# The value products of the second attention with the weights as the stationary side, their results turned back by transposes

## The chip, the cores and the metric

The kernel runs on one core of a Trainium2 chip. The metric is the device time of one execution in microseconds (us). A core has TensorE (PE, with its weight loads shown apart as PEld), VectorE (DVE), ScalarE (ACT) and GpSimd (POOL); the SP queue issues the transfers. The engines run on their own and wait for one another through semaphores.

## The reference, cut to what matters

Two transformer blocks run one behind the other on 512 tokens of width 1024. The change is in the first layer of the second block, which has 8 heads of forgetting attention ("fox") and 8 heads of sparse attention. Each of the latter adds three gated attentions: over compressed keys ("cmp"), over selected key blocks ("slc") and over a window ("win"). At 512 tokens all the selected blocks are taken and the window reaches over everything, so slc and win are causal attentions over all the keys before a token.

```python
s = jnp.einsum('bqhd,bkhd->bhqk', qi, k).astype(jnp.float32) * scale
s = s + ci[..., None] - c[:, :, None, :]
p = masked_softmax(s, kpos[None, :] <= t[:, None])
...
o_s = jnp.einsum('bgrqk,bgqkd->bqgrd', p_s.astype(dt), vg)
...
o_w = jnp.einsum('bgrqk,bkgd->bqgrd', p_w.astype(dt), vw)
return gi[..., 0:1] * o_c + gi[..., 1:2] * o_s + gi[..., 2:3] * o_w
```

The last product of each, probabilities times values, is the one that is changed. In all, a head has 512 queries, up to 512 keys and 64 channels.

## The kernel before

The function `attention` works through 16 steps of two heads each. Steps 0 to 7 alternate cmp and fox (cmp 0, fox 1, cmp 2, fox 3 and so on), steps 8 to 15 alternate slc and win. The order of the work is written out by hand, a loop over the steps on each engine.

On TensorE iteration s does three things. `turn` transposes the probabilities `z` of step s, 128x128 at a time (L2324; the cmp steps' at L2319), in pieces of four: five pieces in a fox, slc or win step, two in a cmp step. They go to two banks of PSUM in turn, and a piece waits until the piece two before it has been copied out. ACT copies pieces 0 and 2 and DVE copies 1, 3 and 4 into `w_T` (L2199). `scores` computes the scores of step s+2 (L2213 and L2214 for cmp, L2222 to L2224 for the rest). `mix` multiplies step s's turned probabilities `w_T` with the values (L2345, cmp at L2341).

In `mix` the values, 128 keys by 64 channels, are loaded as weights, and up to 512 columns of `w_T` are streamed past them. The two heads of a step use columns 0 to 63 and 64 to 127 of the array, so the result stands in bank 7 by channel: 128 channels by 512 tokens, as the next layer wants it. For slc, mix(s) leaves its sum in the bank, and the win step behind it adds onto it.

On DVE iteration s masks and lowers the scores of step s+1 (`lower`, L2261, on 128x512 down to 128x128), adds a win step's result to its block (`add`, L2369), copies its pieces, and computes the softmax weights of step s+1 (`weigh`, L2275 to L2284). On ACT iteration s computes the exponentials of one head of step s+1 (L2293), copies its pieces of step s, copies the result of step s-1 out of bank 7 (`keep`, L2399, fox and cmp), computes the exponentials of the other head and scales its share of both (L2394). At the end of iteration 2 ACT and DVE also split a weight panel into high and low halves (L234, L243). POOL scales the rest of `z` (L2435).

Weights, values and probabilities are in float32. The kernel's source has a matmul once; the trace shows two records (passes) for each float32 matmul and one for a transpose.

Of the kernel before, what the change touches and what calls it, by code (L numbers as in the profile page):

```python
# [22 lines left out]
P = 128  # L23
# [2096 lines left out]
def attention(k, a, heads, f):  # L2120
# [18 lines left out]
    for s, (kind, _) in enumerate(steps):  # L2139
        first_piece.append(len(pieces))  # L2140
        for i in range(2 if kind == "cmp" else len(piece_parts)):
            eng = ("act", "dve")[i] if kind == "cmp" else "act" if i in by_act else "dve"
            done[eng] += 1
            pieces.append((s, i, eng, done[eng]))
    out_bank, turn_bank = 7, 5
# [3 lines left out]
    def pieces_of(s):  # L2149
        return range(first_piece[s], first_piece[s + 1] if s + 1 < n_steps else len(pieces))  # L2150

    def first_of_head(s):
        return steps[s][0] != "win"

    def last_of_head(s):
        return steps[s][0] != "slc"
# [4 lines left out]
    heads_before = [sum(last_of_head(x) for x in range(s)) for s in range(n_steps + 1)]  # L2161
# [4 lines left out]
    top, total, weight = (f.sb(s, [P, slots, TT]) for s in ("top", "total", "weight"))  # L2166
    early_z = heads[:, 6, 0:2 * TT * 32].rearrange("p (e c) -> p e c", e=2)
# [69 lines left out]
    def lower(dve, u):  # L2237
# [4 lines left out]
        if s >= slots // 2:  # L2242
            dve.wait_ge(turned, first_piece[s - slots // 2 + 1])
# [53 lines left out]
    def rest(block, parts, last_panel):  # L2297
# [5 lines left out]
        def _(pe):  # L2303
            def turn(n):
# [22 lines left out]
            def mix(s, j):  # L2327

                kind, i = steps[s]
                if kind == "cmp" and j:  # L2330
                    return
                if j == 0:
                    for n in pieces_of(s)[-2:]:
                        pe.wait_ge(out_of_bank[pieces[n][2]], pieces[n][3])
                    if first_of_head(s) and heads_before[s]:
                        pe.wait_ge(kept, heads_before[s])
                first, final = first_of_head(s) and j == 0, last_of_head(s) and j in (0 if kind == "cmp" else TT - 1,)
                for e in range(2):
                    out = ps[rows_of(e), out_bank, :]
                    if kind == "cmp":  # L2340
                        last = pe.matmul(out, a.vc[:, i // 2, :], w_T[0:32, e, 0:T], start=first, stop=final)  # L2341
                        continue
                    v = {"fox": a.fv[:, j, (2 * i + e) * HD:(2 * i + e + 1) * HD] if kind == "fox" else None,
# [934 lines left out]
```

## Time and profile before

| | |
|---|---|
| three runs | 1986.31 us median (1984.85 to 1991.64) |
| the profiled execution | 1989.59 us, of which its span is 1987.9 us |
| TensorE, busy share of the span | 95% |
| VectorE, ScalarE, GpSimd, busy share | 46%, 38%, 11% |
| the 16 steps | from about 975 to 1115 us of the span |

The profile gives starts in us from the start of the span. A row of the timeline merges neighbouring instructions of one line: its second column reaches from the start of the first to the end of the last, and a record of TensorE reaches to where its result lands, so that records overlap. How fast they follow is read from starts.

### The profile page before, as it was taken

The numbers are of one execution on the slowest core, as the hardware profiler recorded it, in microseconds if no ns is written. First come the engines' busy times: TensorE is split into PE (matmuls) and PEld (weight loads), VectorE is DVE, ScalarE is ACT, GpSimd is POOL, SyncE is SP. The second block draws the span as 40 slices with busy tenths as digits, with TensorE's granted clock in tenths as the row PEclk, the third lists the DMA queues.
The fourth block names the chain that finished last, engine by engine and source line by source line (L and its number), as shares of the span: only waits on it lengthen the run. The fifth ranks groups of instructions, "written<-read, shape, count | busy, mean of one in ns | idle before, by whom it ended". The sixth has DMA issues, their size and how long they took to land. (4 is left out here: it accounts for less than half of the span.)

```text
span 1987.9 us, 32845 instructions
## 1 busy us (share of the span) xinstructions
PE 1893.6 (95%) x13761; PEld 1546.7 (78%) x13761; DVE 917.6 (46%) x1352; ACT 747.3 (38%) x1259; POOL 223.0 (11%) x305
## 2 busy tenths in 40 slices
PE   7999988789999999999979899999999999999998
PEld 6777777657888888778856687888889888888887
DVE  5346666555433344376358464334322453343223
ACT  6533444243321332254468453222222452222222
POOL 3013665100000000000234100000310000000000
PEclk9999999999999999999879999999999799999999
DMA  5322000012322322453100023322233113232221
GB/s 180 106 65 64 4 4 3 11 43 85 104 87 91 100 85 96 99 115 100 43 22 1 22 68 103 102 89 89 86 107 101 43 43 106 85 99 82 85 92 68
DMA packets 152068, 147.97 MB, mean 74 GB/s; under 512 B 13532, under 2 KB 149882, under 8 KB 151930
## 3 DMA queue, kind: packets, MB, share of 16 engines
q1 hardware_dynamic: 151804, 145.91, 23.6%
q8 instruction: 109, 1.79, 0.4%
q14 instruction: 29, 0.24, 0.0%
q10 hardware_dynamic: 126, 0.04, 0.0%
HBM read 143.84 MB, written 2.10 MB: 73 GB/s over the span
## 5 line engine op out<-in xcount | busy, mean ns | idle before, releaser
L243 DVE TENSOR_TENSOR weight_low<-weight_ring,weight_high 128x2048 fp32r<-128x2048 f32 (+2 forms) x141 | 301.1, 2136 | 486.0 <-ACT weight_high L234 485.9
L234 ACT CAST weight_high<-weight_ring 128x2048 fp32r<-128x2048 f32 (+2 forms) x141 | 249.8, 1773 | 322.9 <-PE psum L263 321.8
L261 PE MATMUL psum<-tail_operand_high,weight_high 128*128 128x512 f32 (+1 forms) x768 | 292.7, 381 | 6.4 <-DVE tail_operand_low L2762 5.7
L262 PE MATMUL psum<-tail_operand_low,weight_high 128*128 128x512 f32 (+1 forms) x768 | 290.4, 378 | 0.0
L263 PE MATMUL psum<-tail_operand_high,weight_low 128*128 128x512 f32 (+1 forms) x768 | 290.4, 378 | 0.0
L261 PE MATMUL psum<-tail_hidden_high,weight_high 128*128 128x512 f32 (+1 forms) x520 | 183.2, 352 | 2.5 <-DVE tail_hidden_low L3208 2.5
L263 PE MATMUL psum<-tail_hidden_high,weight_low 128*128 128x512 f32 (+1 forms) x520 | 182.7, 351 | 0.0
L262 PE MATMUL psum<-tail_hidden_low,weight_high 128*128 128x512 f32 (+1 forms) x520 | 182.5, 351 | 0.0
L261 PEld LDWEIGHTS psum<-tail_operand_high,weight_high 128*128 128x128 f32 x768 | 145.3, 189 | 38.0 <-DVE tail_operand_low L2762 5.2
L262 PEld LDWEIGHTS psum<-tail_operand_low,weight_high 128*128 128x128 f32 x768 | 145.5, 189 | 29.7 <-issue 0.5
L263 PEld LDWEIGHTS psum<-tail_operand_high,weight_low 128*128 128x128 f32 x768 | 145.5, 189 | 29.4
L261 PE MATMUL psum<-middle_operand_high,weight_high 128*128 128x512 f32 (+1 forms) x392 | 156.2, 398 | 0.8 <-DVE middle_part L1737 0.8
L263 PE MATMUL psum<-middle_operand_high,weight_low 128*128 128x512 f32 (+1 forms) x392 | 155.4, 396 | 0.0
L262 PE MATMUL psum<-middle_operand_low,weight_high 128*128 128x512 f32 (+1 forms) x392 | 155.3, 396 | 0.0
L261 PE MATMUL psum<-middle_hidden_high,weight_high 128*128 128x512 f32 x320 | 128.1, 400 | 4.6 <-DVE middle_hidden_low L1613 4.6
L262 PE MATMUL psum<-middle_hidden_low,weight_high 128*128 128x512 f32 x320 | 128.0, 400 | 0.0
L263 PE MATMUL psum<-middle_hidden_high,weight_low 128*128 128x512 f32 x320 | 127.8, 399 | 0.0
L261 PEld LDWEIGHTS psum<-tail_hidden_high,weight_high 128*128 128x128 f32 x520 | 98.3, 189 | 17.4 <-issue 2.7
L262 PEld LDWEIGHTS psum<-tail_hidden_low,weight_high 128*128 128x128 f32 x520 | 98.4, 189 | 14.7
L263 PEld LDWEIGHTS psum<-tail_hidden_high,weight_low 128*128 128x128 f32 x520 | 98.2, 189 | 14.5
L261 PEld LDWEIGHTS psum<-middle_operand_high,weight_high 128*128 128x128 f32 (+1 forms) x392 | 73.4, 187 | 19.7 <-DVE middle_part L1737 1.2
L2863 ACT CAST tail_hidden_high<-tail_gate 128x512 fp32r<-128x512 f32 x44 | 27.3, 621 | 162.0 <-DVE tail_gate L2891 162.0
(431 smaller groups left out, 3173.5 us busy)
## 6 DMA issues: line engine op xcount, KB each, us to landing
weight_ring<-in_w_ff SPq DMA_DIRECT2D x32, 1024.0 KB, 5.2
weight_ring<-in_ffn_w_gate SPq DMA_DIRECT2D x22, 1024.0 KB, 5.3
weight_ring<-in_ffn_w_up SPq DMA_DIRECT2D x22, 1024.0 KB, 5.3
weight_ring<-in_ffn_w_down SPq DMA_DIRECT2D x16, 768.0 KB, 4.4
weight_ring<-in_rw_in SPq DMA_DIRECT2D x11, 1024.0 KB, 5.3
weight_ring<-in_ffn_w_down SPq DMA_DIRECT2D x16, 640.0 KB, 3.9
weight_ring<-in_attn_w_in SPq DMA_DIRECT2D x9, 1024.0 KB, 5.4
weight_ring<-in_w_out SPq DMA_DIRECT2D x4, 1024.0 KB, 5.1
```

Of the source, the lines that this page charges most:

```text
L234: act.copy(self.w_hi[:, slot, 0:n], self.ring[:, slot, 0:n]).then_inc(self.panel_high, 1)
L243: dve.tensor_tensor(self.w_lo[:, slot, 0:n], self.ring[:, slot, 0:n], self.w_hi[:, slot, 0:n], ALU.subtract).then_inc(self.panel_low, 1)
L261: pe.matmul(out, w_hi, x_hi, start=start, stop=False)
L262: pe.matmul(out, w_hi, x_lo, start=False, stop=False)
L263: return pe.matmul(out, w_lo, x_hi, start=False, stop=stop)
L2863: act.copy(t.hidden_hi[:, i - 1 + m, :], gate[:, at, :]).then_inc(high, 1)
```

## The change

The two sides of the product trade places for the fox, slc and win steps. `mix` now loads a 128x128 part of `w_T` (128 keys by 128 tokens) as weights and streams the 64 channels of the values past it, once for each of the 10 pairs of a token tile and a key tile on or below the diagonal and for each of the two heads. The result stands in bank 7 by token: 128 tokens by 4 tiles of 128 channels. A step's sums are closed with the step, so slc and win meet no longer in the bank: ACT copies an slc step's result to `out_rows` (the tile `rstd`), and DVE adds the win step's to it.

The results of the 4 fox and the 4 win steps are then turned back to channels by four transposes each (`turn_rows`), which TensorE does in the next iteration, between `scores` and `mix`, and copied (fox, ACT, `keep_block`) or added (win, DVE, `add_block`) into their block. These pieces take a place of their own among the two PSUM banks of the pieces. cmp steps keep their form.

```diff
+        if s and steps[s - 1][0] in ("fox", "win"):
+            eng = "act" if steps[s - 1][0] == "fox" else "dve"
+            done[eng] += 1
+            pieces.append((s, "rows", eng, done[eng]))
...
+            def turn_rows(s):
+
+                n = rows_piece(s)
+                if n is None:
+                    return
+                pe.wait_ge(kept, s + 1)
+                _, _, who, shows = pieces[n - 2]
+                pe.wait_ge(out_of_bank[who], shows)
+                for t in range(TT):
+                    last = pe.transpose(ps[:, turn_bank + n % 2, t * P:(t + 1) * P], out_rows[:, t * P:(t + 1) * P], k.ident[:])
+                last.then_inc(turned, 1)
...
-                    last = pe.matmul(out[:, j * P:T], v, w_T[:, e, w_at[j]:w_at[j] + T - j * P], start=first, stop=final)
...
+                    for tile in range(TT):
+                        for e in range(2):
+                            at = ((2 * i + e) if kind == "fox" else i // 2) * HD
+                            for j in range(tile + 1):
+                                c = w_at[j] + (tile - j) * P
+                                last = pe.matmul(ps[:, out_bank, tile * P + e * HD:tile * P + (e + 1) * HD], w_T[:, e, c:c + P],
+                                                 v[:, j, at:at + HD], start=j == 0, stop=j == tile)
...
-                for j in range(TT):
-                    mix(s, j)
+                if s:
+                    turn_rows(s - 1)
+                mix(s)
+            turn_rows(n_steps - 1)
...
+                    dve.tensor_tensor(out_rows, ps[:, out_bank, :], out_rows, ALU.add).then_inc(kept, 1)
+
+            def add_block(s):
+                if steps[s][0] == "win":
+                    n, block = rows_piece(s), heads[:, block_of(s), :]
+                    dve.wait_ge(turned, n + 1)
+                    dve.tensor_tensor(block, ps[:, turn_bank + n % 2, :], block, ALU.add).then_inc(out_of_bank["dve"], 1)
...
+                    act.copy(heads[:, block_of(s), :] if steps[s][0] == "cmp" else out_rows, ps[:, out_bank, :]).then_inc(kept, 1)
+
+            def keep_block(s):
+                n = rows_piece(s)
+                if steps[s][0] == "fox":
+                    act.wait_ge(turned, n + 1)
+                    act.copy(heads[:, block_of(s), :], ps[:, turn_bank + n % 2, :]).then_inc(out_of_bank["act"], 1)
```

The order of the instructions on TensorE around an slc step's product, before (the names are result, streamed side, weights; the shape is that of the result):

```order
L2223 MATMUL psum<-attn_all_ks_high,attn_all_nq 128x256
L2224 MATMUL psum<-attn_all_ks_low,attn_all_nq 128x256
L2345 MATMUL psum<-attn_w_T,attn_all_vs 64x512 x2
L2345 MATMUL psum<-attn_w_T,attn_all_vs 64x384 x2
L2345 MATMUL psum<-attn_w_T,attn_all_vs 64x256 x2
L2345 MATMUL psum<-attn_w_T,attn_all_vs 64x128 x2
L2324 MATMUL psum<-identity,attn_z 128x128 x20
```

The same place in the changed kernel, behind a win step:

```order
L2226 MATMUL psum<-attn_all_ks_high,attn_all_nq 128x256
L2227 MATMUL psum<-attn_all_ks_low,attn_all_nq 128x256
L2316 MATMUL psum<-identity,rstd 128x128 x4
L2359 MATMUL psum<-attn_all_vs,attn_w_T 128x64 x20
L2339 MATMUL psum<-identity,attn_z 128x128 x20
```

Eight matmuls in four pairs have become 20, and the four transposes of the step before stand between the scores and them.

On ACT, the queue before in iteration 6 (a cmp step), from its piece copy on to the first exponentials of iteration 7:

```order
L2199 COPY attn_w_T<-psum 32x512
L2399 COPY mixer_mixed<-psum 128x512
L2293 ACTIVATE attn_z,attn_total<-attn_z,attn_top 128x512
L2293 ACTIVATE attn_z,attn_total<-attn_z,attn_top 128x384
L2293 ACTIVATE attn_z,attn_total<-attn_z,attn_top 128x256
L2293 ACTIVATE attn_z,attn_total<-attn_z,attn_top 128x128
L2394 ACTIVATE attn_z<-attn_z,attn_weight 128x512 x2
L2293 ACTIVATE attn_z,attn_total<-attn_z,attn_top 128x512
```

And the same stretch in the changed kernel:

```order
L2202 COPY attn_w_T<-psum 32x512
L2425 COPY rstd<-psum 128x512
L2296 ACTIVATE attn_z,attn_total<-attn_z,attn_top 128x512
L2296 ACTIVATE attn_z,attn_total<-attn_z,attn_top 128x384
L2296 ACTIVATE attn_z,attn_total<-attn_z,attn_top 128x256
L2296 ACTIVATE attn_z,attn_total<-attn_z,attn_top 128x128
L2417 ACTIVATE attn_z<-attn_z,attn_weight 128x512 x2
L2431 COPY mixer_mixed<-psum 128x512
L2296 ACTIVATE attn_z,attn_total<-attn_z,attn_top 128x512
```

The fox result goes to `rstd` first, and its copy into the block (`keep_block`, L2431) stands behind the scaling and ahead of everything of the next iteration.

On DVE, the last instructions of the 16 steps before, with the first ones of the stage behind them:

```order
L2199 COPY attn_w_T<-psum 128x512 x3
L2369 TENSOR_TENSOR mixer_mixed<-psum,mixer_mixed 128x512
L2453 UNCONDITIONAL_BRANCH
L3204 UNCONDITIONAL_BRANCH
L3208 TENSOR_TENSOR tail_hidden_low<-mixer_mixed,tail_hidden_high 128x512 x8
```

And in the changed kernel:

```order
L2202 COPY attn_w_T<-psum 128x512 x3
L2383 TENSOR_TENSOR rstd<-psum,rstd 128x512
L2389 TENSOR_TENSOR mixer_mixed<-psum,mixer_mixed 128x512
L2487 UNCONDITIONAL_BRANCH
L3238 UNCONDITIONAL_BRANCH
L3242 TENSOR_TENSOR tail_hidden_low<-mixer_mixed,tail_hidden_high 128x512 x8
```

Between the two additions lie the last four transposes on TensorE.

## Rows read from the trace of the kernel before

**Rows 1.** The page: its span, TensorE's busy time, and the last chain by engine.
```profile
span 1987.9 us, 32845 instructions
...
PE 1893.6 (95%) x13761; PEld 1546.7 (78%) x13761; DVE 917.6 (46%) x1352; ACT 747.3 (38%) x1259; POOL 223.0 (11%) x305
...
PE 42%; DVE 1%; ACT 1%; issue 0%; DVEq 0%
```

**Rows 2.** Busy time by stretch; behind POOL the granted clock, DMA share, GB/s.
```profile
975.00:1116.00 141.00, 117.62 (x724) 86.66 (x721) 93.76 (x338) 97.58 (x303) 50.21 (x75) 0.88 0.03 9
997.80:1011.40 13.60, 7.88 (x30) 6.14 (x29) 7.08 (x18) 7.33 (x24) 2.69 (x5) 0.50 0.23 77
1021.70:1028.40 6.70, 5.12 (x22) 4.28 (x21) 3.54 (x12) 4.09 (x19) 0.85 (x2) 0.50 0.00 0
1042.20:1045.50 3.30, 3.30 (x15) 2.94 (x15) 1.39 (x3) 2.44 (x7) 0.00 (x0) 0.50 0.00 0
1045.60:1113.80 68.20, 59.81 (x410) 43.13 (x410) 52.63 (x188) 51.23 (x149) 26.95 (x32) 1.00 0.00 1
1588.30:1595.00 6.70, 6.70 (x62) 6.70 (x62) 1.13 (x3) 5.87 (x17) 0.00 (x0) 1.00 0.01 2
```

**Rows 3.** Timeline of TensorE from win mix 11 to slc mix 12.
```profile
1081.40 2.37 PE L2345 MATMUL psum<-attn_w_T,attn_all_vw 128*64 128x512 f32 x16
1083.71 1.09 PE L2324 MATMUL psum<-identity,attn_z 128*128 128x128 f32 x8
1085.21 0.63 PE L2324 MATMUL psum<-identity,attn_z 128*128 128x128 f32 x4 [0.41 <-ACT attn_w_T L2199]
1086.24 1.06 PE L2324 MATMUL psum<-identity,attn_z 128*128 128x128 f32 x8 [0.40 <-DVE attn_w_T L2199]
1087.06 0.36 PE L2223 MATMUL psum<-attn_all_ks_high,attn_all_nq 128*128 128x256 f32 x1
...
1089.79 0.65 PE L2345 MATMUL psum<-attn_w_T,attn_all_vs 128*64 128x512 f32 x2
```

**Rows 4.** Timeline of ACT and DVE in the same step: the piece copies.
```profile
1084.50 0.56 ACT L2199 COPY attn_w_T<-psum 128x512 f32<-128x512 f32 x1
...
1085.87 0.59 ACT L2199 COPY attn_w_T<-psum 128x512 f32<-128x512 f32 x1 [0.81 <-PE psum L2324]
...
1085.41 0.68 DVE L2199 COPY attn_w_T<-psum 128x512 f32<-128x512 f32 x1
```

**Rows 5.** Timeline of TensorE and ACT behind fox mix 3, and ACT's panel split.
```profile
1013.98 2.38 PE L2345 MATMUL psum<-attn_w_T,attn_all_fv 128*64 128x512 f32 x16
1016.28 1.05 PE L2319 MATMUL psum<-identity,attn_z 128*32 128x128 f32 x8
1017.51 0.28 PE L2213 MATMUL psum<-attn_all_kc_high,attn_all_nq 128*128 128x32 f32 x1 [0.18 <-DVE attn_top L2261]
...
1017.08 0.56 ACT L2199 COPY attn_w_T<-psum 32x512 f32<-32x512 f32 x1
...
999.16 1.88 ACT L234 CAST weight_high<-weight_ring 128x2048 fp32r<-128x2048 f32 x1
```

**Rows 6.** Timeline of TensorE in a later stage: float32 with full-width weights.
```profile
1549.82 3.63 PE L3038 MATMUL psum<-ones,tail_row_squares 128*128 128x1 f32 x32
...
1588.80 0.29 PE L3055 MATMUL psum<-tail_band_before,tail_pool_z 128*128 128x16 f32 x2
1588.94 0.47 PE L3052 MATMUL psum<-tail_band,tail_pool_z 128*128 128x128 f32 x2
1589.25 0.29 PE L3055 MATMUL psum<-tail_band_before,tail_pool_z 128*128 128x16 f32 x2
```

**Rows 7.** Timeline of the last two mixes and of what follows.
```profile
1104.99 2.37 PE L2345 MATMUL psum<-attn_w_T,attn_all_vs 128*64 128x512 f32 x16 [0.99 <-DVE attn_w_T L2199]
...
1111.85 2.37 PE L2345 MATMUL psum<-attn_w_T,attn_all_vw 128*64 128x512 f32 x16 [0.88 <-DVE attn_w_T L2199]
...
1114.26 0.69 DVE L2369 TENSOR_TENSOR mixer_mixed<-psum,mixer_mixed 128x512 f32<-128x512 f32 x1 [2.56 <-PE psum L2345]
```

More of the change, by code:

```diff
@@ L2149, in pieces_of, with rows_piece @@
     def pieces_of(s):
[L2150 to L2156, printed above, removed]
+        return [n for n in range(len(pieces)) if pieces[n][0] == s and pieces[n][1] != "rows"]
+    def rows_piece(s):
+        return next((n for n in range(len(pieces)) if pieces[n][0] == s + 1 and pieces[n][1] == "rows"), None)
     def block_of(s):
         return steps[s][1] + (0 if steps[s][0] == "fox" else FOX_H // 2)
-    heads_before = [sum(last_of_head(x) for x in range(s)) for s in range(n_steps + 1)]
     last_half_out = None
@@ L2166, in attention @@
     top, total, weight = (f.sb(s, [P, slots, TT]) for s in ("top", "total", "weight"))
+    out_rows = k.rstd[:]
     early_z = heads[:, 6, 0:2 * TT * 32].rearrange("p (e c) -> p e c", e=2)
@@ L2242, in lower @@
         if s >= slots // 2:
-            dve.wait_ge(turned, first_piece[s - slots // 2 + 1])
+            dve.wait_ge(turned, pieces_of(s - slots // 2)[-1] + 1)
         if kind == "cmp":
@@ L2325, in turn, with mix @@
                 last.then_inc(turned, 1)
-            def mix(s, j):
+            def mix(s):
                 kind, i = steps[s]
[L2330 to L2343, printed above, removed]
-                         "slc": a.vs[:, j, (i // 2) * HD:(i // 2 + 1) * HD], "win": a.vw[:, j, (i // 2) * HD:(i // 2 + 1) * HD]}[kind]
-                    last = pe.matmul(out[:, j * P:T], v, w_T[:, e, w_at[j]:w_at[j] + T - j * P], start=first, stop=final)
-                if j == TT - 1 or kind == "cmp":
-                    last.then_inc(mixed, 1)
@@ new lines, in mix @@
+                for n in pieces_of(s)[-2:]:
+                    pe.wait_ge(out_of_bank[pieces[n][2]], pieces[n][3])
+                if s:
+                    pe.wait_ge(kept, s)
+                if kind == "cmp":
+                    for e in range(2):
+                        last = pe.matmul(ps[rows_of(e), out_bank, :], a.vc[:, i // 2, :], w_T[0:32, e, 0:T], start=True, stop=True)
+                else:
+                    v = {"fox": a.fv, "slc": a.vs, "win": a.vw}[kind]
+                    for tile in range(TT):
+                        for e in range(2):
+                            at = ((2 * i + e) if kind == "fox" else i // 2) * HD
[3 more added lines that the diff above has]
+                                                 v[:, j, at:at + HD], start=j == 0, stop=j == tile)
@@ L2350, in _ @@
+                last.then_inc(mixed, 1)
             pe.wait_ge(*banks_free)
@@ L2381, in _ @@
                     weigh(dve, u)
+                if s:
+                    add_block(s - 1)
                 if s == 2:
@@ L2396, in keep @@
             def keep(s):
-                if steps[s][0] in ("cmp", "fox"):
+                if steps[s][0] != "win":
                     act.wait_ge(mixed, s + 1)
-                    act.copy(heads[:, block_of(s), :], ps[:, out_bank, :]).then_inc(kept, 1)
+                    before = [n for n in range(len(pieces)) if pieces[n][1] == "rows" and pieces[n][0] <= s]
+                    if before and steps[s][0] != "cmp":
+                        act.wait_ge(turned, before[-1] + 1)
+                    act.copy(heads[:, block_of(s), :] if steps[s][0] == "cmp" else out_rows, ps[:, out_bank, :]).then_inc(kept, 1)
[4 more added lines that the diff above has]
+                    act.copy(heads[:, block_of(s), :], ps[:, turn_bank + n % 2, :]).then_inc(out_of_bank["act"], 1)
             for s in range(n_steps):
@@ L2413, in _ @@
                     scale(2 * s + 3)
+                if s:
+                    keep_block(s - 1)
                 if s == 2:
```

8 lines of the change are left out of this document (5 added, 3 removed).

## The prediction, made before the changed kernel was run

> **What bounds the kernel now.** I read the page first: its last chain runs through TensorE's matmuls, and TensorE is busy for 95% of the span [rows 1]. The 16 steps that the change touches lie in the middle, and behind them comes a long stretch of TensorE work. So what the steps lose or gain at their end should come out at the end of the kernel one for one; I see nothing there that would absorb it.
>
> Inside the steps TensorE is busy for 117.6 of 141 us, DVE and ACT for 94 and 98 [rows 2]. No share decides, so I went to the timeline of one step. The reader is to see a circle in [rows 3]: mix 11 starts at 1081.40, the transposes of step 12 follow at 1083.71 without a wait, two short waits for piece copies come between them (0.41 and 0.40 us), scores run from 1087.06, and mix 12 starts at 1089.79. That is 8.39 us a step, and TensorE is the one that sets it: its idle time is some 1.5 us, all of it in the transposes. The mix fills 1083.71 - 1081.40 = 2.31 us.
>
> In the cmp and fox steps the circle goes through more engines [rows 5]. Fox mix 3 runs from 1013.98 to 1016.28. Behind it the cmp step is transposed, and ACT copies its piece at 1017.08. In ACT's queue this copy stands ahead of the second head's exponentials, its scaling and all that follows, so a late copy makes everything late up to the next fox mix.
>
> **The price of the new product.** A fox, slc or win mix has 8 matmuls now, 16 passes, of which the two heads' run side by side in the two halves of the array. It becomes 20 matmuls, 40 passes, each with 128x128 weights of its own and 64 streamed columns, one after another. The trace of before has no such pass, but it has a shorter and a longer one of the same weights [rows 6]. With 1 streamed column, 32 passes start within 3.63 - 0.25 (the last one's own length, my reading) = 3.4 us: with the first gap short, 0.112 us a pass. With 16 and 128 columns in turn, two passes of each take 1589.25 - 1588.80 = 0.45 us, again 0.112 us a pass. So from 1 to 128 columns on the mean the pass costs the same: the weight load is the limit and the streaming lies under it. 64 columns lie between, and I take 0.112. The mix is then 40 x 0.112 = 4.48 us instead of 2.31: **+2.17 us, twelve times, 26.0 us.**
>
> The bounds: below, a pass costs only its streaming. Before, a head's four matmuls stream 512 + 384 + 256 + 128 = 1280 columns in each of two passes, both heads side by side, in 2.31 us; the new form streams 20 x 64 = 1280 in each of two passes, one after another. By the column that is 2.3 us again, no change. Above, load and streaming don't overlap: 0.112 + 2.31/40 = 0.17 us, 6.8 us a mix, +4.5.
>
> Here a rule of the Trainium skill speaks against my sum. "TensorE: Matmul & The Clock Gate", section "Back-to-back issue gap", lists some 25 ns between matmuls of 1 to 64 columns. By it 40 passes would take 1.0 us, shorter than the mix of before. The same page's section "LDWEIGHTS (loading the stationary operand)" charges by the weights' columns, 107 ns for 128; by that one 40 passes take 4.3 us and the sum comes out some 2 us under mine. The rows with 1 and with 16 columns decide for the second.
>
> **What hides a part.** In a step of [rows 3] the first piece is turned at about 1083.71 + 0.44, and a copy starts some 0.2 us behind its last transpose (1085.87 against 1085.21 + 0.44), so ACT could start at about 1084.3; it does at 1084.50 [rows 4], when its exponentials end. These start with the scores' end, not with the mix's, so with a longer mix ACT is early. That gives back 0.2 us. The DVE copy (1085.41) stands behind the addition and costs hardly more than this. Behind fox mixes it is much the same: turned at 1016.28 + 0.44 + 0.2, copied at 1017.08 [rows 5]. For 11 mixes, all but the last: **-2.2 us.** The cmp scores behind a fox mix wait 0.18 us for DVE (1017.51); that wait goes too, but the scores lie beside ACT's chain. The POOL scaling for the next transposes gets 2 us more time; it stays hidden.
>
> **The transposes back.** Four at 0.11 us are 0.44 us, as one piece in [rows 3]. They stand between scores and mix, in iterations 2, 4, 6 (cmp), 8, 10, 12 and 14, and behind mix 15. In the cmp iterations TensorE isn't the late one, and ahead of mix 14 it idles for 0.99 us waiting for a DVE copy [rows 7]; both hide them. Left are 8, 10 and 12: **+1.3 us.** If the cover were gone, the other four would cost 1.8.
>
> **The copies.** ACT's copy of an slc result (steps 8, 10, 12, 14) and DVE's additions into the blocks come while TensorE is in its 4.5 us mix; they delay exponentials that have more than 1 us of slack by then. I cost them at nothing. `keep_block` of a fox step is another thing: ACT's queue has it ahead of the next exponentials, and in iteration 2 ahead of the panel split (999.16, [rows 5]) on which DVE waits; a copy is 0.56 us [rows 4], less some overlap 0.5. In iteration 4 the exponentials wait for DVE anyway, 0.1; in 6, 0.3. **+0.9 us.** Unhidden in all four it would be 2.0.
>
> **The end.** Now mix 15 ends, DVE adds in 0.69 us [rows 7], and the next stage begins. Afterwards DVE adds to `out_rows`, TensorE turns (0.44 and 0.2 to be seen), and DVE adds again: **+1.4 us** with the hand-over.
>
> Sum: 26.0 - 2.2 + 1.3 + 0.9 + 1.4 = **27.4 us.** The profiled execution of before took 1989.6 (a span of 1987.9 and 1.7 around it), which makes 2017.0 for its like; it lay 3.3 us above the median of the runs, so I forecast 1986.3 + 27.4 = **2013.7 us** as median.
>
> **The clock.** TensorE's granted clock is at half (1.2 of 2.4 GHz) in three stretches of the cmp and fox steps, 13.6, 6.7 and 3.3 us long, each entered after cmp scores and waits, and full from 1045.6 to 1113.8 [rows 2]. Of the three, some 13 us of TensorE work lie on the path, so they cost about 6.5 us. The shifted steps will meet the falls and rises elsewhere; I take the same cost and 4 us either way.
>
> **The rivals.** (1) The forecast as summed, with a range of its own of 2008 to 2019: 0.78. (2) The load hides, a pass costs its streaming alone: the mix stays at 2.3 us, and left are 1.3 + 0.9 + 1.4 = 3.6 us, 1990, no measurable change. This is the case of the other side. A pass would have to cost under 0.065 us for the whole to stay within 6 us of before. A still cheaper pass, as by the 25 ns of the skill's page, gains no more than 2.4 us over this, since ACT's copy at 1084.50 holds the transposes. Against it stand both measured passes; 0.07. (3) The clock falls inside the new mixes. For it: they stream less in a given time. Against it: 1588.3 to 1595.0, passes of the same load-bound kind, is at full clock throughout [rows 2]. A mix at half clock takes 9.0 us, 4.5 more; one or two of them are within the range, four make 2032. 0.09. (4) Load and streaming don't overlap: 12 x 4.5 instead of 26.0, some 28 more, 2042; the 0.45 us of [rows 6] speaks against it: 0.04. (5) The half-clock stretches vanish with the fuller TensorE and rival 2 holds as well: 3.6 - 6.5, some 1983, of which only the best end is faster by more than a measurement can tell; 0.02.
>
> **How the numbers follow.** A measurement of this kernel tells about 0.3%, 6 us, from no change. Faster by more: 0.01, the best end of (5). Within: (2) and the rest of (5), 0.08. Slower: the others, 0.91. The range leaves out (2), (5), (4) and the farther half of (3), with a bit of each tail of (1): 2006 to 2022.
>
> **What would show it.** L2359 as 40 records a step, their weight loads 0.11 us apart, some 4.5 us from the first to the next transpose; a step of the slc and win half 10.3 us long instead of 8.4 (10.7 with the transposes back); ACT's first piece copy released by TensorE and no longer by ACT's own work; full clock from step 8 to 15; some 3 us between mix 15 and the next stage. I am wrong if the passes follow faster than 0.1 us, if the clock falls in mixes, or if the tail absorbs the delay.

## The result, and the profile after

The changed kernel takes **2011.74 us** in the median of 4 runs (2010.88 to 2013.14), the kernel before beside it 1987.81 (1984.85 to 1991.64, 4 runs). The ratio is 1.0119, 95% interval 1.0102 to 1.0136: slower by 23.9 us, where 27.4 were forecast, and inside the range of 2006 to 2022. The profiled execution took 2012.13 us, against 1989.59 before.

The page of the changed kernel (span, busy time, last chain by engine) answers to [rows 1]:

```profile
span 2010.4 us, 33512 instructions
...
PE 1918.6 (95%) x14081; PEld 1587.1 (79%) x14081; DVE 922.7 (46%) x1356; ACT 752.3 (37%) x1267; POOL 223.2 (11%) x305
...
PE 41%; DVE 1%; ACT 0%; issue 0%; DVEq 0%
```

TensorE is busy for 25.0 us more with 320 records more, and its share has not moved. The page alone tells the size of the change and nothing of its place; the stretches do. Busy time by stretch of the changed kernel (columns as in [rows 2]), the 16 steps first, then three stretches at half clock, the steps 8 to 15, and all that comes behind:

```profile
975.00:1141.60 166.60, 144.32 (x1051) 128.64 (x1049) 99.52 (x342) 102.30 (x311) 50.06 (x75) 0.92 0.02 8
1001.90:1012.10 10.20, 4.36 (x20) 3.71 (x19) 5.52 (x10) 5.57 (x20) 0.04 (x1) 0.50 0.31 103
1025.80:1032.50 6.70, 5.86 (x23) 4.83 (x22) 3.19 (x11) 3.77 (x19) 0.84 (x4) 0.50 0.00 0
1049.70:1053.00 3.30, 3.30 (x12) 2.91 (x11) 2.46 (x7) 3.25 (x10) 1.86 (x3) 0.50 0.00 0
1053.10:1141.80 88.70, 80.47 (x644) 74.07 (x642) 56.65 (x187) 53.45 (x151) 25.00 (x31) 1.00 0.01 1
...
1142.30:2010.40 868.10, 851.69 (x4196) 712.36 (x4196) 328.97 (x360) 273.79 (x366) 26.79 (x46) 0.99 0.26 84
```

The fifth row is full clock from step 7's mix to the end of the steps. Of the three half-clock stretches the first has shrunk from 13.6 to 10.2 us, the others are as long as before.

The steps' clock face is the start of each mix. Before, the first fox mix starts at 991.70 and the next stage at 1116.73, 125.03 us later; after, 991.60 and 1142.30, which is 150.70 us. **The steps took 25.7 us more.** Behind them come the same 4196 records of TensorE in both; the kernel before, in the stretch that answers to the last row above:

```profile
1116.70:1987.90 871.20, 853.56 (x4196) 714.24 (x4196) 329.07 (x360) 273.64 (x366) 26.30 (x46) 0.98 0.26 84
```

871.2 us before and 868.1 after, at a mean granted clock of 0.98 and 0.99: 3.1 us for the same work, by which the profiled spans differ by only 22.5 us. The traces say where they come from: in this stretch the clock is at half for 31.0 us before and for 25.0 us after (the sum of the half-clock stretches of each trace). I don't count that as a gain of the change. In the fourteen profiled executions of this document the stretch takes between 867.7 and 872.9 us with 25.0 to 36.3 us at half clock, with the same 4196 records of TensorE.

The timeline of TensorE from slc mix 10 to slc mix 12 of the changed kernel answers to [rows 3] (its scores are left out):

```profile
1085.31 4.58 PE L2359 MATMUL psum<-attn_all_vs,attn_w_T 128*128 128x64 f32 x40
1089.72 1.04 PE L2339 MATMUL psum<-identity,attn_z 128*128 128x128 f32 x8
1091.10 1.17 PE L2339 MATMUL psum<-identity,attn_z 128*128 128x128 f32 x8 [0.33 <-ACT attn_w_T L2202]
1092.49 0.63 PE L2339 MATMUL psum<-identity,attn_z 128*128 128x128 f32 x4 [0.22 <-ACT attn_w_T L2202]
...
1095.52 4.57 PE L2359 MATMUL psum<-attn_all_vw,attn_w_T 128*128 128x64 f32 x40
...
1105.71 0.60 PE L2316 MATMUL psum<-identity,rstd 128*128 128x128 f32 x4
```

The mix has 40 records and fills 1089.72 - 1085.31 = **4.41 us** (before 2.31). The two waits in the transposes are 0.33 and 0.22 us, before 0.41 and 0.40. I read this as the longer mix giving ACT and DVE the time to be ready. The step from 1085.31 to 1095.52 is 10.21 us; the next, with the four transposes back (1105.71), ends at 1106.14 and is 10.62.

ACT and DVE in the changed kernel, in order: the first piece copy of step 12, which answers to 1084.50 in [rows 4]; ACT's copy of a fox result into its block with the panel split behind it, and DVE's half of that split; then DVE's two additions behind the last mix, which answer to [rows 7]:

```profile
1100.58 0.59 ACT L2202 COPY attn_w_T<-psum 128x512 f32<-128x512 f32 x1 [1.42 <-PE psum L2339]
...
1001.03 0.56 ACT L2431 COPY mixer_mixed<-psum 128x512 f32<-128x512 f32 x1
1001.49 1.89 ACT L234 CAST weight_high<-weight_ring 128x2048 fp32r<-128x2048 f32 x1
...
1003.42 2.29 DVE L243 TENSOR_TENSOR weight_low<-weight_ring,weight_high 128x2048 fp32r<-128x2048 f32 x1 [2.86 <-ACT weight_high L234]
...
1138.39 0.69 DVE L2383 TENSOR_TENSOR rstd<-psum,rstd 128x512 f32<-128x512 f32 x1 [4.79 <-PE psum L2359]
1139.83 0.69 DVE L2389 TENSOR_TENSOR mixer_mixed<-psum,mixer_mixed 128x512 f32<-128x512 f32 x1 [0.75 <-PE psum L2316]
```

The piece copy is released by TensorE, 1.42 us after ACT ran out of work. The last mix starts at 1133.70, so the stretch up to the next stage is 8.60 us instead of 4.88.

The step lengths of all kernels, from mix start to mix start (us, worked out from the starts in the timelines; the last column is from the first fox mix, mix 1, to the next stage, and the kernels are those of the next section):

| kernel | 1 to 3 | 7 to 8 | 8 to 9 | 9 to 10 | 10 to 11 | 15 to next stage | steps in all |
|---|---|---|---|---|---|---|---|
| before | 22.27 | 8.31 | 8.67 | 8.39 | 8.31 | 4.89 | 125.03 |
| after | 23.89 | 10.62 | 10.21 | 10.62 | 10.21 | 8.60 | 150.70 |
| product only | 24.56 | 10.20 | 10.19 | 10.19 | 10.19 | 7.16 | 147.28 |
| turning only | 22.79 | 8.75 | 8.24 | 9.16 | 8.90 | 6.33 | 130.26 |
| 128x64 weights | 22.88 | 8.85 | 8.41 | 9.17 | 8.91 | 6.47 | 130.83 |
| halves side by side | 22.83 | 8.84 | 8.41 | 9.17 | 8.90 | 6.51 | 130.77 |
| halves, no turning | 22.27 | 8.40 | 8.70 | 8.41 | 8.41 | 5.06 | 125.66 |
| halves, copies moved | 22.77 | 8.85 | 8.41 | 8.85 | 8.41 | 6.51 | 128.71 |
| turning only, addition later | 22.80 | 8.75 | 8.22 | 9.20 | 8.24 | 6.32 | 128.98 |
| 128 columns | 23.86 | 10.67 | 10.26 | 10.69 | 10.25 | 8.65 | 151.15 |
| 48 columns | 24.71 | 10.64 | 11.20 | 10.64 | 10.20 | 12.07 | 159.51 |
| 32 columns | 26.55 | 13.05 | 11.40 | 13.04 | 12.60 | 11.02 | 171.65 |
| scores between the pieces | 22.58 | 7.59 | 8.46 | 8.46 | 8.46 | 4.88 | 125.86 |
| scores behind the fourth piece | 22.11 | 7.83 | 8.47 | 9.07 | 8.49 | 4.88 | 126.47 |

### The profile page after: what moved, and what is told of

Read it like the earlier page. It is cut to its first block and busy times, and to the rows that moved or that the text cites. A ratio compares the mean times of both kernels' runs of the same rounds, so it can differ in the third digit from the quotient of the medians.

```text
span 2010.4 us, 33512 instructions
## 1 busy us (share of the span) xinstructions
PE 1918.6 (95%) x14081; PEld 1587.1 (79%) x14081; DVE 922.7 (46%) x1356; ACT 752.3 (37%) x1267; POOL 223.2 (11%) x305
## 5 line engine op out<-in xcount | busy, mean ns | idle before, releaser
L263 PEld LDWEIGHTS psum<-middle_operand_high,weight_low 128*128 128x128 f32 (+1 forms) x392 | 73.4, 187 | 18.4
```

What stands on the lines that cost most here:

```text
L263: return pe.matmul(out, w_lo, x_hi, start=False, stop=stop)
```

## The experiments

### Is it the load or the streaming?

**Twice the streamed columns.** The changed kernel with 128 columns of values past each part; the second half of the result is other heads' and overwritten.

```diff
-    at = ((2 * i + e) if kind == "fox" else i // 2) * HD
+    at = 2 * i * HD if kind == "fox" else 0
...
-    last = pe.matmul(ps[:, out_bank, tile * P + e * HD:tile * P + (e + 1) * HD], w_T[:, e, c:c + P],
-                     v[:, j, at:at + HD], start=j == 0, stop=j == tile)
+    last = pe.matmul(ps[:, out_bank, tile * P:(tile + 1) * P], w_T[:, e, c:c + P],
+                     v[:, j, at:at + P], start=j == 0, stop=j == tile)
```

> The changed kernel with 128 streamed columns in each of the 20 matmuls of a mix instead of 64: the second head's matmuls write over the first head's result, so half of the values' results are wrong. Theory (a pass costs its weight load, 0.110 us, and the streaming lies under it): the 40 passes stay 0.11 us apart, a mix stays at 4.4 us, and the time is that of the changed kernel, 2011.7, within 3 us. Rival (a pass costs by its streamed columns, or load and streaming add up): 0.05 us more a pass, 2.1 us more a mix, some 25 us more, 2037.

Measured: 2013.83 us (2007.96 to 2018.01, 4 runs), ratio 1.012 (1.0099 to 1.0142). Twice the columns, the same time: the steps are 10.7 and 10.25 us in turn instead of 10.62 and 10.21. The timeline shows the mix from 1075.80 to the next transposes at 1080.27, 4.47 us:

```profile
1075.80 4.63 PE L2359 MATMUL psum<-attn_all_vw,attn_w_T 128*128 128x128 f32 x40
1080.27 1.04 PE L2339 MATMUL psum<-identity,attn_z 128*128 128x128 f32 x8
```

So load and streaming don't add up, and the 64 columns of the change lie under the load. Twice as many may be just as long as the load: the mix of before streams 2 x 1280 columns in 2.31 us, which is 0.9 ns a column, and by that 128 columns are some 0.115 us (an estimate).

**Half the streamed columns.** The same kernel with 32 columns (half of each head's result is left out).

> The changed kernel with 32 streamed columns in each matmul instead of 64: half of the channels are left out. Theory (weight load): again 0.11 us a pass and 2011.7 within 3 us. Rival (load and streaming add up): 0.027 us less a pass, 1.1 us less a mix, some 12 us less, 1999.

Measured: 2033.85 us (2030.8 to 2036.31), ratio 1.0226 (1.0209 to 1.0243). Half the streaming makes the kernel *slower* by 22 us, and neither theory said so. Stretch and timeline of this kernel:

```profile
1050.00:1160.00 110.00, 106.07 (x679) 96.55 (x676) 61.61 (x211) 60.32 (x171) 28.07 (x34) 0.78 0.00 1
```

```profile
1108.16 4.55 PE L2359 MATMUL psum<-attn_all_vw,attn_w_T 128*128 128x32 f32 x40
...
1151.32 6.62 PE L2359 MATMUL psum<-attn_all_vw,attn_w_T 128*128 128x32 f32 x40 [0.83 <-DVE attn_w_T L2202]
```

The mean granted clock from step 7 to 15 is 0.78, a mixture of the two levels (1.2 and 2.4 GHz), where the changed kernel has 1.00. A mix that stays at full clock is as long as with 64 columns (4.55 us from first start to last end, against 4.57), one in which the clock falls is up to 6.6 us (L2359 of mix 15; mix 8 takes 4.9). The pass is no cheaper with half the columns; what was lost is the clock.

**Three quarters of them.** To see whether that had been near: 48 columns (a quarter of each head's result is left out).

> The changed kernel with 48 instead of 64 channels streamed past each 128x128 part (a quarter of each head's result is left out). Theory (the load sets the pass, so the time is that of the changed kernel as long as the clock holds): 0.112 us a pass at full clock. What is asked is whether the clock still falls inside the mixes, as it does with 32 columns and not with 64. If it holds: steps 10.2 and 10.6, 2008 to 2014. If it falls as with 32 columns: half clock in most mixes, steps of 11.4 to 13, 2030 or more. Between, some mixes: 2015 to 2028. I expect it to hold or to fall in few: 2008 to 2020.

Measured: 2021.7 us (2020.47 to 2028.89, 4 runs), ratio 1.0179 (1.0158 to 1.02), just above the interval that I gave as likely and in the one of "some mixes". The stretches, and the last mix of its timeline:

```profile
1072.30:1075.00 2.70, 2.70 (x14) 2.17 (x13) 0.69 (x1) 0.71 (x2) 0.00 (x0) 0.50 0.00 0
1133.50:1136.50 3.00, 3.00 (x15) 2.47 (x14) 0.69 (x1) 0.58 (x1) 0.00 (x0) 0.50 0.00 0
1140.40:1150.80 10.40, 7.19 (x33) 6.63 (x32) 2.13 (x4) 1.40 (x3) 0.24 (x1) 0.50 0.00 1
1079.00:1129.00 50.00, 47.03 (x375) 43.21 (x374) 36.93 (x127) 34.04 (x99) 15.02 (x19) 1.00 0.00 1
```

```profile
1138.82 7.66 PE L2359 MATMUL psum<-attn_all_vw,attn_w_T 128*128 128x48 f32 x40 [0.83 <-DVE attn_w_T L2202]
```

From mix 9 to 13 the clock is full and the steps are 10.2 and 10.6 us, as with 64 columns. Behind mix 14 it is at half, and most of mix 15 is run there (7.66 us from first start to last end, against 4.65 in the changed kernel). Ahead of those two mixes TensorE has no scores to compute. The clock is also at half for 3.4 us right behind mix 8 (first row), and that step is 11.20 us instead of 10.21. The rest of the loss is in the fox steps, 3.15 us from mix 1 to mix 7 (0.8 of it from mix 1 to 3, 24.71 us instead of 23.89), where the half-clock stretches are 13.7, 13.7 and 6.8 us long.

**Half the load.** The changed kernel with 64 tokens of each part as weights (128x64; the other half of the tokens is left out).

```diff
-    last = pe.matmul(ps[:, out_bank, ...], w_T[:, e, c:c + P], ...)
+    last = pe.matmul(ps[0:HD, out_bank, ...], w_T[:, e, c:c + HD], ...)
```

> The changed kernel with 64 of the 128 tokens of each weight tile loaded, so 128x64 weights: the results of half of the tokens are left out. The number of matmuls, passes and streamed columns stays. Theory (weight load, by its columns): a pass costs 0.055 us, a mix 2.2 to 2.4 us as before the change, and what is left is the turning back with its copies: 3 to 5 us above before, some 1992. Rival (a price by the pass, whatever its weights): a mix stays at 4.4 us and the time at 2011.7.

Measured: 1995.71 us (1990.05 to 1998.44, 10 runs), ratio 1.0035 (1.0024 to 1.0046). Forty passes of half the load take 2.48 us (1076.28 to the transposes at 1078.76) instead of 4.41:

```profile
1076.28 2.54 PE L2359 MATMUL psum<-attn_all_vs,attn_w_T 128*64 128x64 f32 x40
1078.76 1.09 PE L2339 MATMUL psum<-identity,attn_z 128*128 128x128 f32 x8
```

With the runs above: twice the streaming changed next to nothing, half the load brought the mix down to 56%. It is 0.062 us a pass, and by the 0.9 ns a column above the 64 columns alone are some 0.058 us (an estimate), so here load and streaming may be equally long; whether a still smaller load would gain anything was not tried. The time is 7.2 us over the kernel before (1988.52), the steps 5.8, where 3 to 5 were expected.

**The full result, in halves.** 80 passes with 128x64 weights, the two halves of a part's tokens going to columns 0 to 63 and 64 to 127 of the array.

```diff
+    for half in range(2):
-        last = pe.matmul(ps[:, out_bank, ...], w_T[:, e, c:c + P], ...)
+        last = pe.matmul(ps[rows_of(half), out_bank, ...],
+                         w_T[:, e, c + half * HD:c + (half + 1) * HD], ...)
```

> The changed kernel, nothing left out, with each 128x128 weight tile loaded as two of 128x64, one for each half of the array, each with its own matmul over the same 64 streamed columns: 40 matmuls and 80 passes a mix. Theory (weight load by columns) in two forms: if the two halves load and stream side by side, as the two heads do before the change, a pair costs 0.055 us, a mix 2.3 us, and the time is some 1992; if they load one after another, a pair costs 0.11, a mix 4.4 us, and the time stays at 2011.7. Rival (a price by the pass): 80 passes of 0.11 us are 8.8 us a mix, some 2064.

Measured: 1995.74 us (1987.95 to 1998.01, 6 runs), ratio 1.0028 (1.0011 to 1.0044). The timeline of TensorE:

```profile
1074.89 2.55 PE L2360 MATMUL psum<-attn_all_vs,attn_w_T 128*64 128x64 f32 x80
1077.37 1.09 PE L2339 MATMUL psum<-identity,attn_z 128*128 128x128 f32 x8
1079.29 1.06 PE L2339 MATMUL psum<-identity,attn_z 128*128 128x128 f32 x8 [0.83 <-ACT attn_w_T L2202]
```

80 records in 2.48 us: two half loads side by side cost what one costs alone. So the same token form costs 2.48 - 2.31 = 0.17 us a mix over before instead of 2.10. But a wait of 0.83 us for ACT stands there which before was 0.41, and the steps are 9.17 and 8.90 us. The steps take 5.7 us over before in all, the median 7.2 (before 1988.52), and so 3.7 us over the 1992 that I expected: the turning back costs more behind short mixes than I had in the sum.

### The change in two parts

**The product only**: the token form of the product with nothing kept by token or turned back, slc and win sums meeting in the bank (the result stays by token, so the block is laid out otherwise).

> The kernel before with the new product alone: 20 matmuls with 128x128 weights of w_T, slc and win summed in the bank as before, no turning back and none of the copies that come with it, so the block gets its results by token instead of by channel. Theory (the product's price makes nearly all of the change): 12 mixes of 4.41 instead of 2.31 us are 25.2, less 0.2 to 0.25 us each for copies that no longer wait for ACT, 22.6: 2010. Rival (the turning back and its hand-overs carry a large part): 2000 or less.

Measured: 2011.98 us (2009.54 to 2013.94, 4 runs), before 1987.95; ratio 1.0112 (1.0096 to 1.0127). The steps take 22.3 us more, each 10.19 to 10.21 from 7 on.

**The turning only**: channel product as before, whose result is kept, turned and added as in the change (so the block holds other values).

> The changed kernel with the product of before (8 matmuls a mix by channel), but all of the turning back, copies and waits kept, so the block gets its results turned once too often. Theory (the mix of 4.4 us hides the additions and copies into the block, the short one doesn't): 1.4 at the end, 1.3 for transposes, 0.9 for ACT's copies, and now some 0.8 us in each of the 3 steps behind a win step in which DVE's addition stands ahead of the lowering: 5 to 7 us above before, some 1993. Rival (they are hidden by other work whatever the mix): 3.6 above, 1991. Rival (they carry much of the change by themselves): 12 or more above.

Measured: 2001.32 us (1992.62 to 2002.72, 5 runs), ratio 1.0066 (1.005 to 1.0081). The profiled execution is the 1992.62, with the steps 5.2 us longer. The other four took 1996 to 2003 at a mean granted clock of 0.974 to 0.977, against its 0.979; its trace can't show what they did. By the median, 13.4 us over before (1987.95), this falls to the last rival, by the steps to the theory.

The medians of the two parts don't add up to that of the change (24.0 and 13.4 against 23.9), so I go by the steps of the profiled executions: 22.3 and 5.2 make 27.5, and the change has 25.7. The turning costs 3.4 us behind the long mixes and 5.2 behind the short ones. What is late behind the short ones stands in the turning kernel's timelines of TensorE and DVE (the first row lies in a step of 9.17 us, the others in the one of 8.90 behind it):

```profile
1087.16 0.63 PE L2339 MATMUL psum<-identity,attn_z 128*128 128x128 f32 x4 [0.78 <-ACT attn_w_T L2202]
...
1096.57 1.06 PE L2339 MATMUL psum<-identity,attn_z 128*128 128x128 f32 x8 [1.00 <-ACT attn_w_T L2202]
...
1092.27 0.69 DVE L2387 TENSOR_TENSOR mixer_mixed<-psum,mixer_mixed 128x512 f32<-128x512 f32 x1 [0.65 <-PE psum L2316]
1092.88 0.68 DVE L2264 CUSTOM_DVE_ANT_0 attn_z<-psum,attn_dist 128x512 f32<-128x512 f32 x1
```

At 1092.27 DVE adds a block, having waited for the transposes back, and the lowering (L2264) starts behind it at 1092.88, though its scores were finished before the transposes. I read that this makes ACT's exponentials and then its piece copy late (the wait of 1.00 us at 1096.57); the next run tests it.

**The addition later.** The turning kernel with `add_block` behind the first lowering of the next iteration.

```diff
                 for u in ahead:
                     lower(dve, u)
+                    if s > 1 and u % 2 == 0:
+                        add_block(s - 2)
+                if s == n_steps - 1:
+                    add_block(s - 2)
...
-                if s:
-                    add_block(s - 1)
```

> The kernel that only turns (channel product left as before, results copied to rows and turned by the transposes as in the change), with DVE's addition into the block moved from the end of an iteration to behind the first lowering of the next. Theory (behind a win step the addition waits for the transposes and holds up the lowering, by which the step grew from 8.39 to 9.17 us): the steps 1074 to 1101 that were 9.17 fall to 8.6 to 8.9, those of 8.90 stay, since there ACT's copy of the slc result ahead of its exponentials is the late one; the next stage begins 1 us earlier than 1121.5. Rival (the four transposes and the piece's place in the banks are the price): 9.0 to 9.2 as before. Time: 1991 if the unprofiled runs follow the profiled span this time, 2000 if the lower mean clock of the other runs of the turning kernel comes again; this run also tells whether that extra 9 us belongs to the turning.

Measured: 1991.26 us (1987.54 to 1994.19, 11 runs), ratio 1.0014 (1.0004 to 1.0024). The mechanism is there and I had put it to the wrong steps: those of 8.90 us fell to 8.24, those of 9.17 stayed (9.18 to 9.20). An addition at the end of a step makes the step *behind* it long. The other kind is ACT's, in the same kernel:

```profile
1079.95 0.59 ACT L2425 COPY rstd<-psum 128x512 f32<-128x512 f32 x1
...
1082.75 0.18 DVE L2280 RECIPROCAL attn_weight<-attn_total 128x4 f32<-128x4 f32 x1 [0.46 <-ACT attn_z L2296]
```

The copy of the slc result delays the second head's exponentials, DVE waits 0.46 us for their total, and its lowering, which is next in its queue, starts late. The executions near 2002 of the turning kernel did not come again here, on another chip. On the chip of the turning kernel the kernel before took 1985.91 to 1990.7 us at 0.978 to 0.980, so the chip alone doesn't explain them; whether that place of the additions does is open.

**Halves without turning.** The product-only kernel with halves (the result by token again).

> The kernel before with the token product alone, its 128x128 weights cut into two halves of 64 tokens that go to the two halves of the array; no rows are kept by token or turned back (the result is left by token, so the block's layout differs). Theory (the load of full-width weights is the whole price of the product, and what two halves side by side still cost over before is the transposes back and the copies around them): the mix is 2.33 us, as with the halves and the turning, every step is as long as before (8.3 to 8.4 us in the slc and win half), the next stage begins within 1 us of 1116.7, and the time is 1986 to 1990. Rival (the halves themselves slow the steps, since 80 loads keep some queue full): steps 8.8 to 9.2, 1994 to 1997.

Measured: 1986.49 us (1983.8 to 1989.89, 10 runs), before 1988.62; ratio 0.9993 (0.9983 to 1.0002). The steps take 125.66 us against 125.03. With halves the token product costs nothing that the medians can tell, as the theory said; the profiled steps hold 0.6 us more.

**Halves, both copies moved.** The full change in halves, `add_block` as above, and ACT's copy of an slc result behind the second head's exponentials.

```diff
-                if s:
+                if s and steps[s - 1][0] != "slc":
                     keep(s - 1)
                 if ahead:
                     exps(act, 2 * s + 3)
+                if s and steps[s - 1][0] == "slc":
+                    keep(s - 1)
+                if ahead:
```

> The full change with halves side by side (two loads of 128x64 a part) and with both late copies moved: DVE's addition into the block behind the first lowering of the next iteration, ACT's copy of an slc result behind the second head's exponentials. Theory (with the halves the product costs what it did, and what is left of the turning between steps 8 and 13 is these two copies, 0.66 and about 0.7 us a step, and four transposes every second step): the steps are 8.24 and 8.7 to 8.8 us in turn instead of 8.90 and 9.17, the next stage begins near 1120 instead of 1122.4, and the time is 1989 to 1992, 1.5 to 4 us over before. Rival (moving them only makes another copy late): the steps stay near 9, 1993 to 1996.

Measured: 1994.0 us (1987.38 to 1995.78, 6 runs), before 1988.88; ratio 1.0023 (1.0008 to 1.0038). By the median this falls to the rival, by the steps rather to the theory. TensorE from win mix 9 on:

```profile
1079.68 2.55 PE L2360 MATMUL psum<-attn_all_vw,attn_w_T 128*64 128x64 f32 x80
1082.16 1.09 PE L2339 MATMUL psum<-identity,attn_z 128*128 128x128 f32 x8
1083.59 0.63 PE L2339 MATMUL psum<-identity,attn_z 128*128 128x128 f32 x4 [0.33 <-ACT attn_w_T L2202]
1084.51 1.09 PE L2339 MATMUL psum<-identity,attn_z 128*128 128x128 f32 x8 [0.30 <-DVE attn_w_T L2202]
...
1088.01 0.60 PE L2316 MATMUL psum<-identity,rstd 128*128 128x128 f32 x4
1088.53 2.55 PE L2360 MATMUL psum<-attn_all_vs,attn_w_T 128*64 128x64 f32 x80
```

The waits are 0.33 and 0.30 us, and the steps are 8.41 and, with the four transposes, 8.85 (without the copies moved 8.90 and 9.17). All steps take 3.7 us over before. Of these 0.6 belong to the halves (125.66 against 125.03, the run above) and 3.1 to the turning (128.71 against 125.66), for which the prediction had 3.6 (transposes 1.3, `keep_block` 0.9, the end 1.4). The median is 5.1 over before, 1.4 more than the steps explain; its executions went from 1987.38 at a mean clock of 0.984 to 1995.78 at 0.979, and I leave the 1.4 to that scatter without having shown it.

### Can TensorE's waits be filled?

Before, TensorE waits twice in a step's transposes [rows 3], some 0.8 us in all. Two orders of the kernel before put scores there, from step 8 on.

**Scores between the pieces.** Transposes 0 and 1, a score tile, 2, two tiles, 3 and 4, the other five.

> The kernel before, nothing left out, with the scores of step s+2 put between the pieces of transposes from step 8 on (first group of scores behind piece 1, the second behind piece 2, the rest behind piece 4). Theory (TensorE's circle sets the slc and win steps, and its 0.4 + 0.4 us waits for piece copies are its only slack): the waits are filled, some 0.7 us a step less in 6 steps, 4 us less, 1983.5. Rival (DVE's lowering or POOL's scaling is the next to be late): within 1 us of before. Rival (the wait for DVE's lowering now comes ahead of pieces 2 to 4 and makes them late): 3 or more us slower.

Measured: 1986.35 us (1982.99 to 1988.93, 11 runs), before 1987.95; ratio 0.9988 (0.9979 to 0.9997). The steps are 8.46 us, no shorter, and all of them 125.9 against 125.0, so that the 1.6 us in the medians don't come from them. A new wait took the place of the old ones (TensorE of this kernel):

```profile
1075.40 0.39 PE L2223 MATMUL psum<-attn_all_kw_high,attn_all_nq 128*128 128x256 f32 x1 [1.00 <-DVE attn_top L2262]
```

The scores write the banks that DVE is still lowering.

**Scores behind the fourth piece**, ahead of the fifth, when that lowering is over.

> The kernel before with, from step 8 on, the last piece of transposes put behind the first three score tiles instead of ahead of them. Theory (TensorE's second wait in the transposes, 0.30 to 0.40 us a step, is the only thing that scores can cover without meeting DVE's lowering, which ends at about 1076.5 in a step whose transposes begin at 1075.4): the wait of 1.00 us for the lowering that the earlier interleaving ran into is gone, the steps are 8.0 to 8.1 us instead of 8.39, and the time 1983 to 1985. Rival (DVE's or ACT's chain of copies, weights and lowering is as long as TensorE's, so that it takes over at once): steps of 8.3 to 8.4, 1986.

Measured: 1988.77 us (1981.3 to 1989.63, 11 runs), before 1988.62; ratio 0.9993 (0.9983 to 1.0004). The theory was wrong and the rival right in kind: another chain takes over, and the steps are 8.5 and 9.1 us in turn, longer than the 8.3 to 8.4 it named. Four rows of this kernel, TensorE, DVE and ACT:

```profile
1083.03 0.63 PE L2325 MATMUL psum<-identity,attn_z 128*128 128x128 f32 x4 [1.11 <-ACT attn_w_T L2199]
...
1077.25 0.69 DVE L2199 COPY attn_w_T<-psum 128x512 f32<-128x512 f32 x1 [0.91 <-PE psum L2325]
...
1079.34 0.68 DVE L2262 CUSTOM_DVE_ANT_0 attn_z<-psum,attn_dist 128x512 f32<-128x512 f32 x1
...
1080.13 0.72 ACT L2294 ACTIVATE attn_z<-attn_z,attn_top 128x512 f32<-128x512 f32 x1 [0.40 <-DVE attn_top L2262]
```

DVE waits 0.91 us for the fifth piece, which TensorE now turns behind the scores; from that copy on it works without a wait through its weights to the lowering. ACT's exponentials wait for the lowering, and TensorE's transposes at 1083.03 wait 1.11 us for ACT's copy. So the piece turned later comes back to TensorE as a later copy, through all three engines. That reading rests on this trace alone. No order tried here beats the kernel before by more than 0.12%.

## Why the prediction was right, point by point

| step of the prediction | predicted | measured |
|---|---|---|
| the product, 12 mixes | +26.0 | +25.2 (12 x (4.41 - 2.31)) |
| what hides a part | -2.2 | -3.0 (product only: 22.25 instead of 25.2) |
| transposes back in 8, 10, 12 | +1.3 | +1.3 (0.43, 0.43 and 0.42) |
| `keep_block` | +0.9 | +0.7 (0.5, 0.0 and 0.2 in the turning kernel) |
| the end | +1.4 | +1.4 (8.60 - 7.16; 6.33 - 4.89) |
| sum in the steps | +27.4 | +25.7 |

**The price of a pass** was read from 1 and from 16 and 128 columns [rows 6], and held in between. The load sets it: 2.10 us a mix instead of 2.17, since a mix of 40 passes fills 4.41 us rather than 4.48 (4.41/40 is 0.110). The rule of the Trainium skill, "TensorE: Matmul & The Clock Gate", section "Back-to-back issue gap", that put 25 ns to matmuls of up to 64 columns, was 4 times under it; its section "LDWEIGHTS (loading the stationary operand)" with 107 ns, 4.3 us a mix, came within 3% of the measured 4.41. The Trainium skill says in the first of these two sections that its figures by streamed columns are for a single matmul and at few columns leave the weight loads out, so it was no rule for a mix in which each pass loads new weights, and I should not have set it against the sum. Halving the load (2.48 us) and doubling the streaming (4.47 us) show the load as a cause and not as a fit.

**What hides a part** was mis-sized: 3.0 instead of 2.2, read from the product-only kernel. That it is ACT's copies which no longer wait is my reading of the waits; no run moved them alone. I had also put TensorE's idle time at some 1.5 us a step, where the rows show two waits of 0.41 and 0.40; the sum didn't use it. The steps of 8.31 us gave back the 0.2 of the forecast (10.19 against 8.31 + 2.10 = 10.41), those of 8.39 gave 0.3, and the one from 8 to 9, which had been 8.67, gave 0.6. From 7 to 15 that is 2.4; the rest is from the fox steps, where it can't be told apart from the clock.

**The transposes and the copies.** The transposes back cost their 0.43 us where I had put them and nothing in 14. "I cost them at nothing" of the slc copy and the additions was right with the 4.4 us mix as the cover that I had named. The runs with short mixes show the price without it: 0.3 us in every second step for ACT's copy (9.17 to 8.85), 0.5 to 0.7 in the others for DVE's addition (8.90 to 8.41, or to 8.24 in the turning kernel). `keep_block` cost its 0.5 in iteration 2: DVE's half of the panel split waited 2.86 us for ACT where it had waited 2.38, in the turning kernel as in the changed one. The changed kernel over the product-only one takes 0.68 us more from mix 1 to mix 7, the same total, but as -0.67, +0.94 and +0.41 where I had 0.5, 0.1 and 0.3; why they fall so, beside the clock, is open.

**The end** grew by 1.4 us as summed, but the sign I named for it was wrong by my own sum: from mix 15's end to the next stage it was 2.57 us before [rows 7], so 4.0 and not "some 3 us" was to be expected, and it is 4.2 (8.60 less the 4.41 of a mix).

**The clock** was "same cost, 4 us either way". The step from mix 1 to mix 3 grew by 1.62 us instead of 2.47 (2.17 - 0.2 + 0.5), with its half-clock stretch at 10.2 us and not 13.6. With the product alone this step is 24.56 us, and its half-clock stretch is again as long as before:

```profile
1001.10:1014.80 13.70, 8.16 (x31) 6.95 (x32) 6.48 (x16) 6.41 (x21) 3.32 (x8) 0.50 0.23 77
```

The kernel with 128 streamed columns repeats the changed one, 23.86 us with 10.2 us at half clock:

```profile
1002.70:1012.90 10.20, 4.39 (x19) 3.76 (x20) 5.27 (x10) 5.72 (x20) 0.29 (x1) 0.50 0.31 103
```

So in this step the clock seems to have given back more than `keep_block` took; this rests on three traces, not on a run that changes the clock alone. The 3.1 us behind the steps are the scatter between executions told above. The medians are 23.9 us apart, 1.8 less than the steps.

**The forecast of 2013.7** came closer than its sum. The sum was 27.4 us and the measured difference 23.9: 1.7 of the 3.5 us are in the steps, the other 1.8 outside them. It was added to 1986.3, and the kernel before took 1987.81 beside the changed one; these 1.5 us of luck leave the median only 2.0 us off.

**The rivals.** (2) and (5) fell with the first row of L2359. (4) needed 0.17 us a pass. (3) did not happen, but was nearer than the 0.09 said: I had argued from 1588.3 to 1595.0 [rows 2], a stretch of load-bound passes at full clock, and the runs with 48 and 32 columns have load-bound passes at half clock, 10 and 22 us slower than the changed kernel. That one stretch at full clock was no proof for passes with another share of streaming. The work behind the steps absorbed nothing that can be told from its scatter of 5 us.

## What to carry to other kernels

When the two sides of a product trade places, count the weight loads and not the columns: float32 with 128x128 weights cost 0.11 us a pass here at full clock, whether 32, 64 or 128 columns streamed past it, and the same product came out even only when the loads were cut into halves that run side by side. An edit that is free behind a long TensorE piece (a copy, an addition) can cost 0.3 to 0.7 us a step once that piece is shortened; look at what stands behind it in its own queue. And a wait of TensorE for another engine is not free time if that engine's own loop is as long: filling it made another wait, twice.

## What the runs showed of the hardware

- Fewer streamed columns made the same 40 passes slower: with 64 columns the mean granted clock from step 7's mix to the end of the steps was 1.00, with 32 columns 0.78 (1050 to 1160 us), and the kernel took 22 us more.
- With these weights the price of streaming lies under that of the load and doesn't add to it: 40 passes take 4.41 us with 64 columns and 4.47 with 128.
- Two 128x64 halves load and stream side by side: 80 records in 2.48 us, as many us as 40 of one half alone.
- Executions of one kernel differ by their granted clock: "scores behind the fourth piece" took 1989.4 us at 0.980 and 1981.3 at 0.984.
